# First feed-forward chunk of a two-block transformer step: both halves of the tokens in one product, four banks

## The reference

```python
u = rms_norm(h, g_mlp[i])
h = h + jnp.square(jax.nn.relu(u @ w_ff1[i])) @ w_ff2[i]
ple_gate = jax.nn.sigmoid(rms_norm(h, g_ple[i]) @ w_ple_gate[i])
h = h + ple_gate * (p[i] @ w_ple_proj[i])
```

## Time and profile before

| what | value |
|---|---|
| median of 3 runs | 824.3 us (824.13 to 824.35) |
| the profiled execution | 823.81 us |
| its span | 822.1 us |
| PE busy | 812.8 us, 99% |
| DVE busy | 629.3 us, 77% |
| ACT busy | 462.9 us, 56% |
| mean granted TensorE clock | 0.998 |

### The profile page before, as it was taken

One profiled execution on the slowest core, in us unless ns is written; L12 is line 12 of the kernel. 1 busy time (PEld: TensorE's weight loads), 2 busy tenths in 40 slices (PEclk: granted clock), 3 DMA queues, 4 the chain that ended last, 5 costly groups with the idle time before them and its releaser, 6 DMA issues.

```text
span 822.1 us, 12294 instructions
## 1 busy us (share of the span) xinstructions
PE 812.8 (99%) x4272; PEld 677.7 (82%) x4272; DVE 629.3 (77%) x965; ACT 462.9 (56%) x751; POOL 61.9 (8%) x89
## 2 busy tenths in 40 slices
PE   9999999999999999999999999999999999999996
PEld 7897777898888888877978877888888888888885
DVE  5567777687888898878878997456796877677776
ACT  6657765466555555568544466446346654455444
POOL 2100000110011110301510000010000000000000
PEclk9999999999999999999999999999999999999999
DMA  9867435779999999543965574555544666655641
GB/s 302 275 198 237 136 126 182 251 273 405 346 335 340 319 323 336 191 120 106 272 213 143 164 218 137 171 154 153 180 154 128 201 189 209 196 178 172 209 130 52
DMA packets 89213, 173.15 MB, mean 211 GB/s; under 512 B 6553, under 2 KB 37001, under 8 KB 89041
## 3 DMA queue, kind: packets, MB, share of 16 engines
q1 hardware_dynamic: 83008, 142.56, 54.2%
q0 software_dynamic: 6000, 29.93, 10.5%
q10 hardware_dynamic: 160, 0.07, 0.0%
HBM read 170.42 MB, written 1.06 MB: 209 GB/s over the span
## 4 chain that ended last, share of the span: by engine, by line
PE 95%; DVE 2%; issue 1%; ACT 1%; POOLq 0%; POOL 0%; ACTq 0%; DVEq 0%
PE B L1709 19%; PE B L1711 19%; PE B L1710 19%; PE B L1772 15%; PE B L1775 8%; PE B L1852 2%; PE B L1787 2%; PE B L1882 2%; PE B L1860 1%; PE B L1873 1%; PE B L2126 1%; PE B L1790 1%; DVE w_lo L1032 1%; PE B L1818 0%; PE B L1809 0%
## 5 line engine op out<-in xcount | busy, mean ns | idle before, releaser
L1032 DVE TENSOR_TENSOR w_lo<-raw,w_hi 128x1024 fp32r<-128x1024 f32 (+3 forms) x154 | 184.8, 1209 | 49.4 <-ACT w_hi L569 47.9
L1709 PE MATMUL B<-w_hi,xT 128*128 128x512 f32 (+3 forms) x536 | 209.5, 391 | 0.0
L569 ACT ACTIVATE w_hi<-raw 128x1024 fp32r<-128x1024 f32 (+3 forms) x154 | 157.5, 1030 | 88.6 <-PE B L1711 74.6
L1711 PE MATMUL B<-w_hi,xT 128*128 128x512 f32 (+3 forms) x536 | 204.5, 381 | 0.0
L1710 PE MATMUL B<-w_lo,xT 128*128 128x512 f32 (+3 forms) x536 | 204.1, 381 | 0.0
L1709 PEld LDWEIGHTS B<-w_hi,xT 128*128 128x128 f32 x536 | 100.8, 188 | 20.7 <-issue 2.2
L1711 PEld LDWEIGHTS B<-w_hi,xT 128*128 128x128 f32 x536 | 100.7, 188 | 19.8
L1710 PEld LDWEIGHTS B<-w_lo,xT 128*128 128x128 f32 x536 | 100.9, 188 | 17.4
L1772 PE MATMUL B<-xT,w_hi 128*128 128x512 f32 x320 | 100.5, 395 | 0.0
L982 ACT ACTIVATE w_hi<-raw 128x1024 fp32r<-128x1024 f32 x60 | 62.2, 1055 | 42.5 <-PE B L1775 30.9
L1302 DVE TENSOR_TENSOR w_lo<-raw,w_hi 128x1024 fp32r<-128x1024 f32 x56 | 67.2, 1221 | 21.7 <-ACT w_hi L787 20.8
(11 more groups left out here) (270 smaller groups left out, 1071.4 us busy)
## 6 DMA issues: line engine op xcount, KB each, us to landing
raw<-in_w_in_dram SPq DMA_DIRECT2D x79, 512.0 KB, 3.9
raw<-in_w_ff_dram SPq DMA_DIRECT2D x64, 512.0 KB, 7.4
Z<-in_w_ada_dram POOLq DMA_DIRECT2D x32, 768.0 KB, 7.6
raw<-in_w_ffn_gate_dram SPq DMA_DIRECT2D x44, 256.0 KB, 3.4
raw<-in_w_ffn_up_dram SPq DMA_DIRECT2D x44, 256.0 KB, 4.1
raw<-in_w_ffn_down_dram SPq DMA_DIRECT2D x20, 512.0 KB, 4.3
raw<-in_w_mix_out_dram SPq DMA_DIRECT2D x8, 512.0 KB, 3.7
raw<-in_w_ple_gate_dram SPq DMA_DIRECT2D x8, 512.0 KB, 4.3
```

Source lines behind the costliest of these rows:

```text
L569: nc.scalar.activation(w_hi[:, u % SPLIT, :, 0:n], raw[:, st.slot[u], :, 0:n], ACT.Copy).then_inc(hi_done, 1)
L1032: nc.vector.tensor_tensor(w_lo[:, u % SPLIT, :, 0:n], raw[:, st.slot[u], :, 0:n], w_hi[:, u % SPLIT, :, 0:n].bitcast(F32), ALU.subtract).t ...
L1709: nc.tensor.matmul(bank, xh, wh, start=start, stop=False)
L1711: return nc.tensor.matmul(bank, xl, wh, start=False, stop=stop)
```

## The change

Chunk 0 is multiplied by `unit_T2` in banks 0 to 3 instead of by `unit_T` in banks 2 and 3, and its values leave the banks as in the loop: two copies by ACT, two additions by DVE, two relus by ACT. The additions stand ahead of `first_piece(3)` in DVE's order. The loop's counts of additions rise by two. `unit_T` goes.

```diff
             split_to(U_FF + 3 + AHEAD)
-            for b in range(2):
-                if b == 0:
-                    act.wait_ge(sem("first_bank"), 1)
-                else:
-                    act.wait_ge(units_used, U_FF + 4)
-                nc.scalar.activation(nat[:, 0, b, :], B[:, 2 + b, :], ACT.Relu).then_inc(sem("relu"), 1)
+            hidden_minor(U_FF + 4, 1)
+            relu2(2)
             square(2)
...
-                relu2(j * 2)
+                relu2(j * 2 + 2)
...
             split_to(U_FF + 3 + AHEAD)
-            first_piece(3)
...
+            hidden_sums(1)
+            first_piece(3)
             hidden_lo(0, 1)
             hidden_lo(1, 2)
...
-                        hidden_sums(j * 2 - 1)
+                        hidden_sums(j * 2 + 1)
...
-            def unit_T(u, xh, xl, kt0, banks, first, last):
...
                 pe.wait_ge(lo_done, u + 1)
-                unit_T(u, sT_hi, sT_lo, 2 * kp, (2, 3), kp == 0, kp == 3)
+                unit_T2(u, sT, 2 * kp, kp == 0, kp == 3)
                 if kp == 0:
                     pe.wait_ge(sem("h_done"), 4)
                     transposes((6, 7), half_rows(h, 1), "wt_done")
```

## The result

The changed kernel took 826.85 us (median of 8 executions, 825.42 to 827.37), the kernel before 824.03 us (8, 823.66 to 824.35): a ratio of 1.003, with a 95% interval of 1.0021 to 1.0038. It is slower by more than the 0.2% that a measurement of this kernel can tell. The time lies in the stated range, and 0.85 us above the forecast. The forecast of the difference was +1.7 us, and +2.8 us was measured.

A forecast was written before the change was run, and what follows sets the result against it. PE was taken to bound the kernel; the longer way out of the banks, net of the products' saving, starts chunk 1 1.69 us later, so +1.7 on 824.3 gives 826.0 us (+0.21%), range 825.2 to 827.0 us.

The forecast's parts named there:

- The bound: Whole kernel: PE is 95% of the last chain, so a microsecond on PE is one in the result.
- later wait: Rival after chunk 1: a PE wait independent of PE takes the 1.7 us back, 823.9 us at best; 8 in 100.
- The products: Chunk 0 on PE: 64 joined matmuls replace 96, saving 0.36 us.
- The aside: Chunk 0's products: at 2.5 ns a matmul the saving is 0.08 us and the forecast 0.02 us later.
- The wait: Between chunks 0 and 1: PE waits some 2.0 us for relu, set by DVE's queue; chunk 1 starts 1.69 us later.
- What else moves: Behind the boundary: later splits, `w_ada` pieces and loads cost nothing; the fourth unit's split has 3.6 us to spare.
- second wait in chunk 1: Rival: the fourth unit's split or the loop's first additions fall behind, another 0.5 to 1 us, 826.7 us; 7 in 100.
- The rival of the clock: Behind PE's 2.0 us idle gap the clock falls, adding 1.5 us: 827.5 us; 5 in 100.
- The step that failed: In the clock rival: PE had so far idled 0.8 us, during which the clock stayed at 1.00.
- a sign of being wrong: Chunk 1's start: PEclk below 1.00 behind the gap would show the prediction wrong.
- The range: Whole time: 825.2 to 827.0 us, leaving out most of the clock and second-wait rivals.
- The chances: Whole result: 0.55 slower, 0.44 same, 0.01 faster, with 0.2% or 1.65 us as the line.

The follow-up runs named there:

- e5: The changed kernel unaltered, executed a second time: median 825.77 us over 10 executions.
- e4: The kernel before with only chunk 0's joined products, relu straight from banks 0 and 2, no copies or additions (not the whole computation): 823.57 us.
- e1: The changed kernel with eight products of ones on PE filling the gap between chunk 0 and chunk 1: 825.41 us.
- e3: The changed kernel with the fourth piece of `w_ada` back ahead of the two additions on DVE: 828.00 us.
- e7: The changed kernel with DVE's two additions ahead of the third of three splits, PE's wait still on the relus: 825.17 us.
- e11: The changed kernel unaltered, executed a third time: median 825.66 us over 11 executions.
- e2: The changed kernel with PE's wait for chunk 1's banks put on the additions instead of the relus, in the loop too: 824.63 us.
- e8: The changed kernel with DVE's additions ahead of the third split and PE's wait on the additions instead of the relus: 824.07 us.
- e6: The kernel before with only a wait added, ACT holding chunk 0's first relu until the fourth `w_ada` piece is summed: 826.08 us.
- e10: The same kernel as e3, executed again on one chip with e9: 828.06 us.
- e9: The kernel of e3 with twelve products of ones on PE filling the gap: 826.26 us.

## Why the prediction was right or wrong

- **The bound** was right: the delay of the boundary is found again behind it, 3.40 us at the first `w_ff2` product, 3.38 at 355.86, 3.3 in the span, so no later wait takes any of it back. In the profiled execution it is twice the 1.7 us forecast for every PE start from there on, and the clock makes the difference; in e5, with the clock held, it is 197.08 - 195.12 less the offset of 0.27, 1.69 us.
- **The products** were right: 0.36 us forecast, 0.35 measured (e4). By the 2.5 ns a matmul of the Trainium skill ("TensorE: Matmul & The Clock Gate", Back-to-back issue gap) the estimate was 0.08 us; the trace does not agree with it here, at 0.35 us for 32 matmuls, 11 ns each. The aside that the forecast would come 0.02 us later by that price was a slip: the first unit's share would be 0.02 in place of 0.09, so 0.07 later.
- **The wait** was right step by step. Every gap in the two chunks belongs to the one wait forecast. With the offset of 0.14 us the steps were due at 182.64 (copy 0), 183.97 (copy 1), 184.24 (addition), 184.95 (relu), 185.72 (PE), and came at 182.57, 183.96, 184.25, 184.96 and 185.74. Its price was forecast as 1.69 us, and where the clock held the two chunks measured 1.69 more (e1, e5). That DVE's queue sets it and ACT's second copy is next was also right (e3, e7).
- **What else moves** was right to cost nothing: ACT's split for the fourth unit came at 188.18 (due at 188.24), with PE far from needing it, and in e1 PE is busy for all of 185.58 to 198.00, so there is no second wait in chunk 1.
- **The rival of the clock** had the right mechanism and too small a chance. Its price was 1.5 us and 1.57 was measured; but the length of the fall was borrowed from the kernel's first six matmuls, and that it fits so well is in part luck. That those six were slow for the clock is itself read from their pace, for the record of the granted clock says 1.00 there. I gave it 5 in 100; it came in 9 of 29 executions, and in 5 of the first 8, so that the measured median is that of forecast and rival together: 824.03 + 1.69 + 1.57 = 827.3, against executions of 826.83 to 827.37 with a mean of 827.0.
- **The step that failed** is the sentence that PE had idled for at most 0.8 us at a clock of 1.00, which I let count against a fall. It says nothing about 2.0 us, where the clock fell in 10 of 36 executions. Nor do the windows that it cites for the clock hold a wait of PE; the trace does read 1.00 around the one of 0.8 us, at 384.5. The rule of the Trainium skill ("TensorE: Matmul & The Clock Gate", What's actually happening) that an idle PE drops to half its clock holds here: the window behind the gap reads 0.50. The prediction named less than 1.00 behind the gap as a sign of being wrong, and the profiled execution shows it.
- **The time in the range** is luck in part. The range, up to 827.0 us, was meant to leave out the clock's 827.5 us, and the median is a time of fallen executions; two of the first eight, at 827.08 and 827.37 us, lie above the range. The median is 0.65 us below 827.5 and so inside: 0.27 of that is the kernel before, measured at 824.03 and not at 824.3, and the rest is a slightly smaller effect of wait and fall on the whole times. The forecast of 826.0 us itself lies in the empty stretch between the two groups of executions, whose means are 825.6 and 827.0 us.
- **The chances** of slower, 0.55, rested on a forecast that lay on the line of 0.2%. By the sets that were little disturbed by the clock (e5: 1.0024, e11: 1.0025) it lies a little above it even so, but their intervals (1.0014 to 1.0033 and 1.0016 to 1.0034) reach below it.

## What to carry to other kernels

A form of product that saves PE 0.36 us can cost it five times that when its result takes one more step to leave the banks, at a boundary where the next product needs the same banks: cost the way from the last matmul to the freed bank, in the order in which each engine's queue has it, before counting matmuls. Let PE wait for the last reader of the bank and not for what is computed afterwards from the copy, and put that reader ahead of work that has time. A gap of two microseconds or more on a PE that has been busy throughout should be priced twice, once for itself and once with the clock down behind it.

## What the runs showed of the hardware

Over all chips together the clock fell more often behind longer idle gaps: in none of 33 executions with gaps of 0.3 to 1.5 us (e2, e7, e8), in 10 of 36 with 2.0 us (the changed kernel and e6), in 9 of 10 with 2.9 us (e3, e10), and in none of 18 in which products of ones filled the gap (e1, e9). After a fall PE ran dense matmuls at 0.50 (186.50 to 189.00 in the changed kernel), and each fall with a trace cost 1.55 to 1.57 us in the two chunks, after 2.0 us of idleness and after 2.9 us alike (e9 beside e10, e5 beside the changed kernel). For gaps of 2.0 us the share differed from set to set (5 of 8, 1 of 10, 3 of 11, 1 of 7). Of these e5 and e6 ran on one chip and e11 on another, and for the first set no chip is on record; whether chip or chance decides stays open. So does a part of the count by length: that 2.9 us is worse than 2.0 us is seen on one chip (5 of 5 against 3 of 11), while between 1.5 and 2.0 us the chip that ran both shows 0 of 22 against 2 of 17 (e7 and e8, e5 and e6), which could be chance. So does the lone slow execution of e7. A median over a handful of executions can thus be 825.66 or 826.85 us for the same kernel.
